# Four groups in seven-product form per pass of the two FFN output projections, instead of three

## The chip, the cores and the metric

The kernel runs on one core of a Trainium2 chip. The metric is the device time of one execution in microseconds; lower is better. The engines are TensorE (PE; its weight loads are listed as PEld), VectorE (DVE), ScalarE (ACT), GpSimd (POOL) and SyncE (SP, which here issues the weight DMAs).

## The reference

One decoder layer on 256 tokens of width 2048, in float32:

```
x = x + 0.5 * swiglu_ffn(rmsnorm(x), ffn1_w_in, ffn1_w_out)
h = rmsnorm(x); proj = h @ w_in        # two groups of 8 heads: q, k, v, and a forget gate
x = x + concat(dilated_attention(...), forgetting_attention(...)) @ w_out
x = x + 0.5 * swiglu_ffn(rmsnorm(x), ffn2_w_in, ffn2_w_out)

def swiglu_ffn(x, w_in, w_out):
    gate, up = jnp.split(x @ w_in, 2, axis=-1)
    return (jax.nn.silu(gate) * up) @ w_out
```

The hidden width of an FFN is 5504, which is 43 tiles of 128. The change touches only the product with `w_out`, 256 x 5504 by 5504 x 2048, in both FFNs.

## The kernel before

**Arithmetic.** Each float32 operand is split into a rounded part (hi, made by ScalarE's copy to fp32r) and the rest (lo, made by VectorE's subtraction), and every product is three matmuls: hi*hi, hi*lo, lo*hi. Weights come from HBM by DMA into `raw` slots of 8 KB per partition. ScalarE copies a half piece (128 x 1024) to `whi`, VectorE subtracts to get `wlo`, and TensorE uses both. There are four such slots; the unit of this chain is called a half here, and halves are numbered h. ScalarE may split half h only when TensorE has finished half h - 4 (`act_e.wait_ge(weights_used, h - SLOTS + 1)`).

**Output projection (`ffn_out` on each engine).** It runs in two passes of 1024 output columns. A pass is a list of items (`out_items`), one half each, in the same order on all engines. A `plain` item is one of the 43 activation tiles against its two 512 columns for both token blocks: 12 matmuls. A group takes four activation tiles as a 2 x 2 block matrix and computes its products in seven-product (Strassen-Winograd) form, one `form` item of 6 matmuls for each of T1, B11, T3, T2, B21, B22, T4. Four plain tiles cost 48 matmuls, one group 42. Before, each pass has 3 groups and 31 plain tiles. Within a group a plain item stands after B11, after T2 and after B22; `LEADS` says how many plain items stand ahead of each group: (8, 5, 5) in the first pass, (6, 5, 5) in the second.

**Additional work of a group.** VectorE makes four sums of weights in or from the group's two raw pieces (`out_sum`, 128 x 1024 each: T1's after the item two ahead of T1, T3's after T1, T2's after the item behind B11, T4's after the item behind T2). VectorE makes four sums of activations (`group_form_sums`, 128 x 256 each, after the item four ahead of T1), ScalarE rounds them (`group_form_hi`, 128 x 1024, ahead of the split three ahead of T1) and VectorE subtracts (`group_form_lo`). The group's own four activation tiles are split by `group_act_hi` (two ScalarE operations ahead of the split of the item before T1; waits until TensorE has used the previous group's T4) and `group_act_lo`. Each plain tile's activation is split by `act_hi` and `act_lo`, 128 x 256 each, into one of four tile places. At the end of a pass `join` adds the four separate product banks onto x, in steps 0 to 5, one after each item.

**Order.** All of it is written out by hand as program order per engine with semaphores. SyncE issues the loads in the order of `out_loads`; a raw slot is loaded again when `free(n)` says that its last reader is done. The group pieces use raw slots 3 and 4, the plain pieces 0 to 2, and slot 5 holds `sfo`, the split sums of the current group. The sums and their splits are made anew in the second pass. Between the FFNs the token mixer starts with `x_turn` (transposes of x) issued inside the last items of the second pass.

Of the kernel before, what the change touches and what calls it, by code (L numbers as in the profile page):

```python
# [7 lines left out]
P = 128  # L8
# [3 lines left out]
FT = D_FF // P  # L12
# [19 lines left out]
W = 512  # L32
UNITS = -(-D_FF // W)
# [39 lines left out]
PLAIN_TILES = FT - OUT_PLAIN  # L73

# [78 lines left out]
def layer(nc, io, out):  # L153
# [3 lines left out]
    with ctx:  # L157
# [9 lines left out]
        x = sb("x", [P, TB, D_MODEL])  # L167
        xs = sb("xs", [P, KT, 2, SEQ], f32r)
# [49 lines left out]
        place[0] = raw_at + 5 * 4 * W * 4  # L218
        sfo = sb("sfo", [P, 4, 2, 2, P], f32r)
        assert place[0] <= tsum_at  # L220
# [55 lines left out]
        def act_slot(c, k):  # L276
            return divmod((c * PLAIN_TILES + k) % 4, 2)

        def act_count(u, c, k):
            return PLAIN_TILES * (PASSES * u + c) + k - OUT_PLAIN + 1  # L280

# [10 lines left out]
        gs = [gset[:, 1 - c].rearrange("p b (f k t) -> p (b f) k t", f=2, k=2) for c in range(PASSES)]  # L292
# [35 lines left out]
        def _(sp):  # L328
            def free(n):
                for u in range(2):  # L330
# [138 lines left out]
        def _(pe):  # L469
# [112 lines left out]
            def ffn_out(u):  # L582
                for c in range(PASSES):
# [7 lines left out]
                    for i, item in enumerate(OUT_ITEMS[c][:ends]):  # L591
# [16 lines left out]
                        else:  # L608
                            g, f = item[1], item[2]
                            if f == "T1":  # L610
                                pe.wait_ge(gs_ready, group(u, c, g) + 1)
# [9 lines left out]
                            for k in range(2):  # L621
# [3 lines left out]
                                else:  # L625
                                    form_s = ("T1", "T2", "T3", "B22").index(f)
                                    st_hi, st_lo = sfo[:, form_s, k, 0, :], sfo[:, form_s, k, 1, :]
# [154 lines left out]
        def _(act_e):  # L782
# [57 lines left out]
            def act_hi(u, c, k):  # L840
                a, a_in = act_slot(c, k)
                act_e.wait_ge(act_copied, ACT_PAIRS * u + k // 2 + 1)
# [116 lines left out]
            def ffn_out(u):  # L959
                for c in range(PASSES):  # L960
                    for i, item in enumerate(OUT_ITEMS[c]):
# [4 lines left out]
                        if len(ahead) > 3 and ahead[3][0] == "form" and ahead[3][2] == "T1":  # L966
                            group_form_hi(u, c if i + 3 < OUT_LEN else c + 1, ahead[3][1])
# [147 lines left out]
        def _(dve):  # L1115
# [67 lines left out]
            def act_lo(u, c, k):  # L1183
                a, a_in = act_slot(c, k)
                dve.wait_ge(aw_hi_ready, act_count(u, c, k))
                V.tensor_tensor(aw_lo[:, a, a_in, :], act[:, k, :], aw_hi[:, a, a_in, :].bitcast(f32), ALU.subtract).then_inc(aw_ready, 1)
# [7 lines left out]
            def group_form_sums(u, c, g):  # L1194
                G, t, S = group(u, c, g), 4 * g, gs[c]
                A11, A21, A12, A22 = act[:, t:t + 2, 0:P], act[:, t:t + 2, P:2 * P], act[:, t + 2:t + 4, 0:P], act[:, t + 2:t + 4, P:2 * P]
                dve.wait_ge(act_copied, ACT_PAIRS * u + 2 * g + 2)
                dve.wait_ge(act_psum, UNITS * (u + 1) - 1 + c)
# [11 lines left out]
            def group_form_lo(u, c, g):  # L1210
                dve.wait_ge(gs_hi, group(u, c, g) + 1)
                V.tensor_tensor(sfo[:, :, :, 1, :], gs[c], sfo[:, :, :, 0, :].bitcast(f32), ALU.subtract).then_inc(gs_ready, 1)
# [19 lines left out]
            def join(u, c, step):  # L1232
# [10 lines left out]
                if step == 0:  # L1243
                    dve.wait_ge(p1_copied, PASSES * u + c + 1)
                    dve.wait_ge(gs_ready, group(u, c, OUT_GROUPS - 1) + 1)
# [127 lines left out]
            def ffn_out(u):  # L1373
                for c in range(PASSES):
                    t4 = OUT_ITEMS[c].index(("form", OUT_GROUPS - 1, "T4"))
                    for i, item in enumerate(OUT_ITEMS[c]):
# [5 lines left out]
                        if item[0] == "plain":  # L1382
                            k = item[1]
                            act_lo(u, c, k)
# [231 lines left out]
```

## Time and profile before

| | |
|---|---|
| time, median of 3 runs | 1767.82 us (1767.69 to 1769.09) |
| the profiled execution | 1767.65 us, span 1765.8 us |
| PE busy | 1759.1 us, 8062 matmuls |
| DVE busy | 1470.7 us (83%) |
| ACT busy | 1068.2 us (60%) |
| DMA | 350.84 MB, mean 199 GB/s |
| granted TensorE clock | 1.000 |

The span is the time from the first to the last instruction of the profile; the execution's own time is 1.85 us longer. A duration in a timeline is the time from issue to completion of one instruction, and neighbours on an engine overlap: the distance between starts is what an instruction costs a full engine.

### The profile page before, as it was taken

What the parts mean: (1) busy time and instruction counts of PE and PEld (TensorE: products, weight loads), DVE (VectorE), ACT (ScalarE), POOL (GpSimd) and SP (SyncE); (2) the same over time, 40 slices, a digit from 0 to 9 for tenths busy, and PEclk for the clock granted to TensorE, in tenths of its full rate; (3) what the DMA queues carried; (4) which work ended last, traced back from release to release, by engine and by line L of the source; (5) the groups of instructions that cost most, each with busy time, mean ns of one, the idle gap of its engine ahead of it and who ended that gap; (6) DMA issues with size and microseconds to landing.
All of it is one profiled execution on the core that took longest, in us unless ns stands there. A gap on an engine that the chain in (4) does not pass through costs nothing.

```text
span 1765.8 us, 20899 instructions
## 1 busy us (share of the span) xinstructions
PE 1759.1 (100%) x8062; PEld 1468.7 (83%) x8062; DVE 1470.7 (83%) x1624; ACT 1068.2 (60%) x1356; POOL 28.1 (2%) x34
## 2 busy tenths in 40 slices
PE   9999999999999999999999999999999999999999
PEld 7888888888988888888888888888888888988887
DVE  7999999998899998575655655999999999899988
ACT  7666666666666666454545554666666666666564
POOL 0000000000000001100000000000000000000000
PEclk9999999999999999999999999999999999999999
DMA  9655555554645546555455457355555555554662
GB/s 378 227 213 213 199 190 191 191 191 156 249 169 216 223 169 230 184 185 183 155 187 167 167 169 261 125 208 192 211 214 213 214 213 187 198 193 157 238 220 102
DMA packets 156179, 350.84 MB, mean 199 GB/s; under 512 B 5960, under 2 KB 16224, under 8 KB 155952
## 3 DMA queue, kind: packets, MB, share of 16 engines
q1 hardware_dynamic: 153280, 341.36, 54.8%
q0 software_dynamic: 1424, 5.53, 1.0%
q10 hardware_dynamic: 1376, 2.62, 0.4%
q8 instruction: 64, 1.05, 0.2%
q14 instruction: 35, 0.29, 0.0%
HBM read 347.37 MB, written 3.69 MB: 199 GB/s over the span
## 4 chain that ended last, share of the span: by engine, by line
PE 99%; DMA 0%; DVE 0%; ACT 0%; issue 0%; SPq 0%; ACTq 0%; DVEq 0%
PE bank L534 10%; PE bank L536 10%; PE bank L535 10%; PE bank L522 7%; PE bank L524 7%; PE bank L523 7%; PE bank L479 7%; PE bank L481 7%; PE bank L480 7%; PE bank L606 6%; PE bank L605 6%; PE bank L604 6%; PE bank L632 2%; PE bank L631 2%; PE bank L630 2%; PE bank L507 1%
## 5 line engine op out<-in xcount | busy, mean ns | idle before, releaser
L1120 DVE TENSOR_TENSOR wlo<-raw,whi 128x1024 fp32r<-128x1024 f32 (+1 forms) x644 | 764.9, 1206 | 190.3 <-ACT whi L791 185.8
L791 ACT ACTIVATE whi<-raw 128x1024 fp32r<-128x1024 f32 (+1 forms) x644 | 669.7, 1046 | 409.5 <-PE bank L481 191.6
L534 PE MATMUL bank<-whi,xs 128*128 128x512 f32 (+1 forms) x768 | 297.4, 387 | 1.5 <-DVE wlo L1120 1.5
L536 PE MATMUL bank<-whi,xs 128*128 128x512 f32 (+1 forms) x768 | 295.5, 385 | 0.0
L535 PE MATMUL bank<-wlo,xs 128*128 128x512 f32 (+1 forms) x768 | 295.3, 385 | 0.0
L604 PE MATMUL bank<-whi,aw_hi 128*128 128x512 f32 x484 | 188.7, 390 | 0.0
L606 PE MATMUL bank<-whi,aw_lo 128*128 128x512 f32 x484 | 188.4, 389 | 0.0
L605 PE MATMUL bank<-wlo,aw_hi 128*128 128x512 f32 x484 | 188.3, 389 | 0.0
L534 PEld LDWEIGHTS bank<-whi,xs 128*128 128x128 f32 x768 | 144.2, 188 | 29.1 <-issue 2.4
L536 PEld LDWEIGHTS bank<-whi,xs 128*128 128x128 f32 x768 | 144.1, 188 | 27.7
L535 PEld LDWEIGHTS bank<-wlo,xs 128*128 128x128 f32 x768 | 144.2, 188 | 26.8
L479 PE MATMUL bank<-whi,xs 128*128 128x512 f32 x384 | 155.8, 406 | 0.0
L481 PE MATMUL bank<-whi,xs 128*128 128x512 f32 x384 | 150.2, 391 | 0.0
L480 PE MATMUL bank<-wlo,xs 128*128 128x512 f32 x384 | 149.6, 390 | 0.0
L791 ACT ACTIVATE whi<-tsum 128x1024 fp32r<-128x1024 f32 (+1 forms) x80 | 83.0, 1040 | 96.5 <-PE bank L536 64.2
L524 PE MATMUL bank<-whi,sf 128*128 128x512 f32 (+1 forms) x320 | 122.7, 384 | 0.0
L522 PE MATMUL bank<-whi,sf 128*128 128x512 f32 (+1 forms) x320 | 122.7, 384 | 0.0
L523 PE MATMUL bank<-wlo,sf 128*128 128x512 f32 (+1 forms) x320 | 122.7, 384 | 0.0
L1120 DVE TENSOR_TENSOR wlo<-tsum,whi 128x1024 fp32r<-128x1024 f32 (+1 forms) x80 | 94.0, 1195 | 25.7 <-ACT whi L791 25.7
L606 PEld LDWEIGHTS bank<-whi,aw_lo 128*128 128x128 f32 x484 | 90.8, 188 | 18.8
L605 PEld LDWEIGHTS bank<-wlo,aw_hi 128*128 128x128 f32 x484 | 90.9, 188 | 18.8
L604 PEld LDWEIGHTS bank<-whi,aw_hi 128*128 128x128 f32 x484 | 90.8, 188 | 18.7
(195 smaller groups left out, 2579.7 us busy)
## 6 DMA issues: line engine op xcount, KB each, us to landing
raw<-ffn_w_in SPq DMA_DIRECT2D x158, 1024.0 KB, 7.1
raw<-ffn_w_out SPq DMA_DIRECT2D x84, 1024.0 KB, 6.7
raw<-w_in SPq DMA_DIRECT2D x48, 1024.0 KB, 5.0
raw<-w_out SPq DMA_DIRECT2D x16, 1024.0 KB, 5.0
raw<-ffn_w_in SPq DMA_DIRECT2D x16, 768.0 KB, 5.0
x<-x SPq DMA_DIRECT2D x4, 512.0 KB, 11.4
raw<-ffn_w_out SPq DMA_DIRECT2D x4, 512.0 KB, 4.2
xt<-x_turned SPq DMA_DIRECT2D x3, 512.0 KB, 8.6
```

The source lines that it names most:

```text
L479: mm(banks[b][:, 0:w], stationary[:, k, 0, tok], hi, start=k == 0, stop=False, skip_group_check=True)
L480: mm(banks[b][:, 0:w], stationary[:, k, 0, tok], lo, start=False, stop=False, skip_group_check=True)
L481: last = mm(banks[b][:, 0:w], stationary[:, k, 1, tok], hi, start=False, stop=k == k_total - 1, skip_group_check=True)
L522: mm(bank_out[:, 0:w], st_hi, hi, start=start and i == 0 and k == 0, stop=False, skip_group_check=True)
L534: mm(banks[b][:, 0:w], xs[:, k + i, 0, tok], hi, start=starts[b] and k + i == 0, stop=False, skip_group_check=True)
L535: mm(banks[b][:, 0:w], xs[:, k + i, 0, tok], lo, start=False, stop=False, skip_group_check=True)
L536: last = mm(banks[b][:, 0:w], xs[:, k + i, 1, tok], hi, start=False, stop=k + i == last_k, skip_group_check=True)
L604: mm(bank_out[:], st_hi, hi, start=i == 0, stop=False, skip_group_check=True)
L605: mm(bank_out[:], st_hi, lo, start=False, stop=False, skip_group_check=True)
L606: last = mm(bank_out[:], st_lo, hi, start=False, stop=k == FT - 1, skip_group_check=True)
L791: A(whi[:, h % SLOTS, 0:n_el], src, ACT.Copy).then_inc(weights_hi, 1)
L1120: V.tensor_tensor(wlo[:, h % SLOTS, 0:n_el], src, whi[:, h % SLOTS, 0:n_el].bitcast(f32), ALU.subtract).then_inc(weights_lo, 1)
```

## The change

Each pass has four groups and 27 plain tiles. The plain runs ahead of the groups become (4, 3, 2, 2) and (5, 2, 2, 2). The group pieces rotate over raw slots 3, 4 and 5, and a group's first piece is freed by the T4 sum, its second by the split of B22. `sfo` holds the split sums of all four groups and lies in the place of `xs`, which is idle in this stage; sums and splits are made in the first pass only, and the second reads them. `group_form_hi` therefore waits until TensorE has finished the last half of the input product (`weights_used` at OUT[u]). Plain activations are split two tiles at a time (128 x 512) into two places of two tiles, so `act_hi` waits for the tile three before; at the start of the second pass it waits for the last tile of the first. Two `join` steps of the second pass come behind its last item, and the two transposes of x stand behind the last two items.

```diff
-OUT_GROUPS = 3
+OUT_GROUPS = 4
-LEADS = ((8, 5, 5), (6, 5, 5))
+LEADS = ((4, 3, 2, 2), (5, 2, 2, 2))
+PLAIN_PAIRS = -(-PLAIN_TILES // 2)
@@ raw_slot
-            return 3 + q % 2 if q < 0 else (c * ACT_PLAIN + q) % 3
+            return 3 + (c * 2 * OUT_GROUPS + OUT_LOADS[c][i]) % 3 if q < 0 else (c * ACT_PLAIN + q) % 3
@@ layer
-        place[0] = raw_at + 5 * 4 * W * 4
-        sfo = sb("sfo", [P, 4, 2, 2, P], f32r)
+        place[0] = xs_at
+        sfo = sb("sfo", [P, OUT_GROUPS * 4, 2, 2, P], f32r)
@@
-            return divmod((c * PLAIN_TILES + k) % 4, 2)
+            return divmod((c * 2 * PLAIN_PAIRS + k - OUT_PLAIN) % 4, 2)
@@ sync: free(n)
-                        item = ("form", q // 2, "T4") if q < 2 * OUT_GROUPS else ("plain", min(2 * q + 1, FT - 1))
+                        if q < 2 * OUT_GROUPS and q % 2 == 0:
+                            return out_sums, 4 * group(u, c, q // 2) + 4
+                        item = ("form", q // 2, "B22") if q < 2 * OUT_GROUPS else ("plain", min(2 * q + 1, FT - 1))
@@ tensor: ffn_out
-                        if c and u == 0 and i in (OUT_LEN - 4, OUT_LEN - 2):
+                        if c and u == 0 and i >= OUT_LEN - 2:
                             pe.wait_ge(p_joined, 8 + 4)
-                            x_turn(1, (i - OUT_LEN + 4) // 2)
+                            x_turn(1, i - OUT_LEN + 2)
@@ scalar: act_hi(u, c, k)
+                n = min(2, FT - k)
                 if k >= OUT_PLAIN + 4:
-                    act_e.wait_ge(weights_used, out_half(u, c, ("plain", k - 4)) + 1)
+                    act_e.wait_ge(weights_used, out_half(u, c, ("plain", k - 3)) + 1)
                 elif c:
-                    act_e.wait_ge(weights_used, out_half(u, c - 1, ("plain", k - 4 + PLAIN_TILES)) + 1)
+                    act_e.wait_ge(weights_used, out_half(u, c - 1, ("plain", FT - 1)) + 1)
                 else:
                     act_e.wait_ge(weights_used, unit_half(u, UNITS - 1) + B22 + 2)
-                A(aw_hi[:, a, a_in, :], act[:, k, :], ACT.Copy).then_inc(aw_hi_ready, 1)
+                A(aw_hi[:, a, 0:n, :], act[:, k:k + n, :], ACT.Copy).then_inc(aw_hi_ready, 1)
@@ scalar: group_form_hi
-            def group_form_hi(u, c, g):
-                G = group(u, c, g)
-                if g or c:
-                    c0, g0 = (c, g - 1) if g else (c - 1, OUT_GROUPS - 1)
-                    act_e.wait_ge(weights_used, out_half(u, c0, ("form", g0, "B22")) + 1)
-                else:
-                    act_e.wait_ge(weights_lo, OUT[u])
-                act_e.wait_ge(gs_summed, 4 * G + 4)
-                A(sfo[:, :, :, 0, :], gs[c], ACT.Copy).then_inc(gs_hi, 1)
+            def group_form_hi(u, g):
+                act_e.wait_ge(weights_used, OUT[u])
+                act_e.wait_ge(gs_summed, 4 * (OUT_GROUPS * u + g + 1))
+                A(split_sums(g)[:, :, :, 0, :], gs, ACT.Copy).then_inc(gs_hi, 1)
@@ scalar: ffn_out
-                            act_hi(u, c, k)
+                            if (k - OUT_PLAIN) % 2 == 0:
+                                act_hi(u, c, k)
@@ vector: ffn_out
-                                if d == 3:
-                                    group_form_sums(u, c1, g1)
-                                if d == 2:
-                                    group_form_lo(u, c1, g1)
+                                if d == 3 and c1 == 0:
+                                    group_form_sums(u, g1)
+                                if d == 2 and c1 == 0:
+                                    group_form_lo(u, g1)
@@
+                for step in range(OUT_LEN - 1 - T4_ENDS[1], 6):
+                    join(u, 1, step)
```

## Rows read from the trace of the kernel before

**Rows 1.** The page, parts 1 and 2: the engines, and VectorE's share in 40 slices.

```profile
PE 1759.1 (100%) x8062; PEld 1468.7 (83%) x8062; DVE 1470.7 (83%) x1624; ACT 1068.2 (60%) x1356; POOL 28.1 (2%) x34
...
DVE  7999999998899998575655655999999999899988
```

**Rows 2.** The page, part 4: the chain that ended last.

```profile
PE 99%; DMA 0%; DVE 0%; ACT 0%; issue 0%; SPq 0%; ACTq 0%; DVEq 0%
```

**Rows 3.** Windows: stretch, length; PE, PEld, DVE, ACT, POOL, clock, DMA, GB/s; first pass.

```profile
461.30:574.70 113.40, 113.40 (x505) 93.91 (x504) 102.15 (x128) 70.32 (x94) 0.00 (x0) 1.00 0.55 204
```

**Rows 4.** Timeline of TensorE: start us, us, line, operation, tiles.

```profile
461.27 0.39 PE L604 MATMUL bank<-whi,aw_hi 128*128 128x512 f32 x1
...
483.76 0.39 PE L630 MATMUL bank<-whi,sfo 128*128 128x512 f32 x1
...
485.12 0.39 PE L630 MATMUL bank<-whi,aw_hi 128*128 128x512 f32 x1
...
574.20 0.39 PE L604 MATMUL bank<-whi,aw_hi 128*128 128x512 f32 x1
...
574.88 0.39 PE L604 MATMUL bank<-whi,aw_hi 128*128 128x512 f32 x1
```

**Rows 5.** Timeline of ScalarE, first FFN's output; [idle before <-releaser].

```profile
461.53 1.06 ACT L791 ACTIVATE whi<-raw 128x1024 fp32r<-128x1024 f32 x1 [0.71 <-PE bank L536]
...
467.03 1.06 ACT L791 ACTIVATE whi<-raw 128x1024 fp32r<-128x1024 f32 x1 [2.32 <-DMA raw<-ffn_w_out]
...
475.12 1.15 ACT L860 ACTIVATE aw_hi<-act 128x512 fp32r<-128x512 f32 x2
476.16 0.41 ACT L849 ACTIVATE aw_hi<-act 128x256 fp32r<-128x256 f32 x1
...
501.72 1.06 ACT L870 ACTIVATE sfo<-gset 128x1024 fp32r<-128x1024 f32 x1 [3.04 <-DVE gset L1208]
502.68 0.40 ACT L849 ACTIVATE aw_hi<-act 128x256 fp32r<-128x256 f32 x1
502.99 1.04 ACT L791 ACTIVATE whi<-raw 128x1024 fp32r<-128x1024 f32 x1
```

**Rows 6.** Timeline of VectorE, the same stretch.

```profile
461.69 0.61 DVE L1174 SCALAR_TENSOR_TENSOR gset<-bank,rstd,gset 128x384 f32<-128x384 f32 x1
...
463.33 0.42 DVE L1186 TENSOR_TENSOR aw_lo<-act,aw_hi 128x256 fp32r<-128x256 f32 x1
...
475.87 1.22 DVE L1120 TENSOR_TENSOR wlo<-raw,whi 128x1024 fp32r<-128x1024 f32 x1
477.01 1.22 DVE L1220 TENSOR_TENSOR tsum<-raw 128x1024 f32<-128x1024 f32 x1
...
479.62 1.28 DVE L1191 TENSOR_TENSOR aw_lo<-act,aw_hi 128x512 fp32r<-128x512 f32 x2
480.82 1.22 DVE L1393 TENSOR_TENSOR wlo<-tsum,whi 128x1024 fp32r<-128x1024 f32 x1
...
500.08 0.42 DVE L1203 TENSOR_TENSOR gset<-act 128x256 f32<-128x256 f32 x1
...
504.07 1.23 DVE L1120 TENSOR_TENSOR wlo<-raw,whi 128x1024 fp32r<-128x1024 f32 x1 [0.52 <-ACT whi L791]
```

**Rows 7.** Timeline of all engines at the start: TensorE's one wait for VectorE.

```profile
7.61 1.23 DVE L1120 TENSOR_TENSOR wlo<-raw,whi 128x1024 fp32r<-128x1024 f32 x1
...
8.98 0.47 PE L534 MATMUL bank<-whi,xs 128*128 128x512 f32 x1 [1.53 <-DVE wlo L1120]
...
9.28 0.39 PE L535 MATMUL bank<-wlo,xs 128*128 128x512 f32 x1
```

**Rows 8.** Timeline of ScalarE: the squares of x in the second pass.

```profile
592.42 0.62 ACT L816 ACTIVATE gset<-x 128x512 f32<-128x512 f32 x1
...
593.84 1.07 ACT L985 ACTIVATE whi<-raw 128x1024 fp32r<-128x1024 f32 x1
```

**Rows 9.** Timeline of SyncE: three loads issued at the start of the stage.

```profile
455.79 1.39 SPq L353 DMA_DIRECT2D raw<-ffn_w_out  x3
```

More of the change, by code:

```diff
@@ L167, in layer @@
         x = sb("x", [P, TB, D_MODEL])
+        xs_at = place[0]
         xs = sb("xs", [P, KT, 2, SEQ], f32r)
@@ L217, in layer @@
         assert place[0] <= tsum_at
-        place[0] = raw_at + 5 * 4 * W * 4
-        sfo = sb("sfo", [P, 4, 2, 2, P], f32r)
-        assert place[0] <= tsum_at
+        place[0] = xs_at
+        sfo = sb("sfo", [P, OUT_GROUPS * 4, 2, 2, P], f32r)
+        assert place[0] <= forms_at
         place[0] = tsum_at
@@ L276, in act_slot @@
         def act_slot(c, k):
-            return divmod((c * PLAIN_TILES + k) % 4, 2)
+            return divmod((c * 2 * PLAIN_PAIRS + k - OUT_PLAIN) % 4, 2)
         def act_count(u, c, k):
-            return PLAIN_TILES * (PASSES * u + c) + k - OUT_PLAIN + 1
+            return PLAIN_PAIRS * (PASSES * u + c) + (k - OUT_PLAIN) // 2 + 1
         def group(u, c, g):
@@ L290, in pair, with split_sums @@
             return tile.rearrange("p (k f) -> p k f", k=2)
-        gs = [gset[:, 1 - c].rearrange("p b (f k t) -> p (b f) k t", f=2, k=2) for c in range(PASSES)]
+        gs = gset[:, 1].rearrange("p b (f k t) -> p (b f) k t", f=2, k=2)
+        def split_sums(g):
+            return sfo[:, 4 * g:4 * g + 4]
         p_banks = [bank[0:4], bank[4:8]]
@@ L610, in ffn_out @@
                             if f == "T1":
-                                pe.wait_ge(gs_ready, group(u, c, g) + 1)
+                                pe.wait_ge(gs_ready, OUT_GROUPS * u + g + 1)
                                 if g == 0 and c == 0:
@@ L626, in ffn_out @@
                                     form_s = ("T1", "T2", "T3", "B22").index(f)
-                                    st_hi, st_lo = sfo[:, form_s, k, 0, :], sfo[:, form_s, k, 1, :]
+                                    st_hi, st_lo = split_sums(g)[:, form_s, k, 0, :], split_sums(g)[:, form_s, k, 1, :]
                                 hi, lo = whi[:, slot, k * W:(k + 1) * W], wlo[:, slot, k * W:(k + 1) * W]
@@ L840, in act_hi @@
             def act_hi(u, c, k):
+                n = min(2, FT - k)
                 a, a_in = act_slot(c, k)
[L842 removed]
+                act_e.wait_ge(act_copied, ACT_PAIRS * u + (k + n - 1) // 2 + 1)
                 if k >= OUT_PLAIN + 4:
[L844 removed]
+                    act_e.wait_ge(weights_used, out_half(u, c, ("plain", k - 3)) + 1)
                 elif c:
[L846 removed]
+                    act_e.wait_ge(weights_used, out_half(u, c - 1, ("plain", FT - 1)) + 1)
                 else:
                     act_e.wait_ge(weights_used, unit_half(u, UNITS - 1) + B22 + 2)
[L849 removed]
+                A(aw_hi[:, a, 0:n, :], act[:, k:k + n, :], ACT.Copy).then_inc(aw_hi_ready, 1)
             def group_act_hi(u, c, g):
@@ L965, in ffn_out @@
                             act_copy(u, UNITS - 1)
-                        if len(ahead) > 3 and ahead[3][0] == "form" and ahead[3][2] == "T1":
-                            group_form_hi(u, c if i + 3 < OUT_LEN else c + 1, ahead[3][1])
+                        if c == 0 and i + 3 < OUT_LEN and ahead[3][0] == "form" and ahead[3][2] == "T1":
+                            group_form_hi(u, ahead[3][1])
                         if len(ahead) > 1 and ahead[1][0] == "form" and ahead[1][2] == "T1":
@@ L1183, in act_lo @@
             def act_lo(u, c, k):
+                n = min(2, FT - k)
                 a, a_in = act_slot(c, k)
                 dve.wait_ge(aw_hi_ready, act_count(u, c, k))
-                V.tensor_tensor(aw_lo[:, a, a_in, :], act[:, k, :], aw_hi[:, a, a_in, :].bitcast(f32), ALU.subtract).then_inc(aw_ready, 1)
+                V.tensor_tensor(aw_lo[:, a, 0:n, :], act[:, k:k + n, :], aw_hi[:, a, 0:n, :].bitcast(f32), ALU.subtract).then_inc(aw_ready, 1)
             def group_act_lo(u, c, g):
@@ L1192, in group_act_lo, with group_form_sums @@
                                     ALU.subtract).then_inc(ga_ready, 1)
-            def group_form_sums(u, c, g):
-                G, t, S = group(u, c, g), 4 * g, gs[c]
+            def group_form_sums(u, g):
+                G, t, S = OUT_GROUPS * u + g, 4 * g, gs
                 A11, A21, A12, A22 = act[:, t:t + 2, 0:P], act[:, t:t + 2, P:2 * P], act[:, t + 2:t + 4, 0:P], act[:, t + 2:t + 4, P:2 * P]
                 dve.wait_ge(act_copied, ACT_PAIRS * u + 2 * g + 2)
-                dve.wait_ge(act_psum, UNITS * (u + 1) - 1 + c)
+                dve.wait_ge(act_psum, UNITS * (u + 1) - 1)
                 if G:
@@ L1208, in group_form_sums, with group_form_lo @@
                 V.tensor_tensor(S[:, 3], A12, S[:, 1], ALU.subtract).then_inc(gs_summed, 1)
-            def group_form_lo(u, c, g):
-                dve.wait_ge(gs_hi, group(u, c, g) + 1)
-                V.tensor_tensor(sfo[:, :, :, 1, :], gs[c], sfo[:, :, :, 0, :].bitcast(f32), ALU.subtract).then_inc(gs_ready, 1)
+            def group_form_lo(u, g):
+                dve.wait_ge(gs_hi, OUT_GROUPS * u + g + 1)
+                V.tensor_tensor(split_sums(g)[:, :, :, 1, :], gs, split_sums(g)[:, :, :, 0, :].bitcast(f32), ALU.subtract).then_inc(gs_ready, 1)
             def out_sum(u, c, g, f):
@@ L1244, in join @@
                     dve.wait_ge(p1_copied, PASSES * u + c + 1)
-                    dve.wait_ge(gs_ready, group(u, c, OUT_GROUPS - 1) + 1)
+                    dve.wait_ge(gs_ready, OUT_GROUPS * (u + 1))
                     V.tensor_tensor(u2, P6[:], p1s[:], ALU.add).then_inc(p_joined, 1)
@@ L1383, in ffn_out @@
                             k = item[1]
-                            act_lo(u, c, k)
+                            if (k - OUT_PLAIN) % 2 == 0:
+                                act_lo(u, c, k)
                             n = out_piece(u, c, k // 2)
```

## The prediction

> **What bounds the kernel now.** I read the engines' shares first: TensorE is busy for 1759.1 of 1765.8 us, VectorE for 83% over all, but 90% or more in most slices of the FFNs' stages [rows 1]. The chain that ended last is 99% TensorE [rows 2], so a matmul taken out is worth its whole distance to the next, as long as weights arrive in time. Next I took the stage that changes, by its first pass: 113.40 us in which TensorE never rests while VectorE is busy for 102.15 [rows 3]. So VectorE has 10% to spare here, no more. Last come the timelines of the engines, for distances between starts. TensorE: a form item of 6 matmuls takes 485.12 - 483.76 = 1.36 us, three matmuls 0.68, so a plain item of 12 takes 2.72 and a matmul 0.227 [rows 4]. (31 plain and 21 form items make 112.9; the pass has 0.5 more, its six transposes [rows 3].) VectorE: 1.14 for a 1024-wide operation, 0.60 for a 512-wide one [rows 6]. ScalarE: 0.96 and 0.52 [rows 5].
>
> Four latencies decide the rest. TensorE's next item starts at 461.27 and ScalarE, released by the last one, at 461.53: 0.26 [rows 4, 5]. From the start of ScalarE's split to that of VectorE's: 504.07 - 502.99 = 1.08 [rows 5, 6]. From the start of VectorE's split to the first matmul that waited for it: 8.98 - 7.61 = 1.37 [rows 7]. And the round trip of the activation sums: VectorE starts them at 500.08, ScalarE rounds at 501.72 (1.64), its next operation starts 0.96 later, VectorE's next split 1.08 after that: 3.68 in which VectorE does 1.5 us of work [rows 5, 6].
>
> **The saving.** Four passes have each one group more: 6 matmuls less in each, 24 x 0.227 = 5.4 us. ScalarE and VectorE also lose the second pass's activation sums and their splits; neither engine bounds that pass, so this is worth nothing by itself.
>
> **First pass: VectorE becomes the bound.** Between two T1's that are one lead of 2 apart VectorE has 12 splits, 4 weight sums and the split of the activation sums (17 x 1.14 = 19.4), 2.5 pairs of plain activations (1.5), the group's own (1.2) and the round trip (3.7): 25.8 us. TensorE needs 7 x 1.36 + 5 x 2.72 = 23.1. With a lead of 5 it was 20 such operations, eight single tiles of activation (about 0.34 each), 1.2 and 3.7: 30.4 against 31.3, and it just fitted. A lead of 2 does not fit, and four halves of buffer can't carry it, the less as the stage now begins late: ScalarE must wait for the last matmul of the input product before it rounds the first sums, ahead of item 1. The split of item 1 so starts on VectorE 0.26 + 0.96 + 1.08 = 2.3 after the stage begins. From there VectorE has work without a gap. Up to the split of P36 (item 43, the plain tile behind B11 of the last group; behind it come no more sums of activations, and VectorE gets ahead) these are 42 splits, 4 splits of sums, 14 weight sums (60 x 1.14 = 68.4), 10 pairs (6.0), 4 group activations (4.8), 3 round trips (11.0), the SwiGLU of the last unit (1.6 [rows 6]) and 0.6 where it waits for ScalarE: 92.4. TensorE can start P36 at 2.3 + 92.4 + 1.4 = 96.1. Unhindered it would be there after 20 plain and 23 form items and the transposes: 86.2. So 9.9 us are lost per first pass, 19.8 in all. If VectorE did not bind, only waits that begin at TensorE would be left in this pass: 1.0 at item 1 (2.3 + 1.4 - 2.7) and some 2 at each of two groups, 5.0; that is the lower bound. I take 9.9, since every term is a row of this stage.
>
> **Start of the second pass.** The first pair of activations now waits for P42, the item just ahead. ScalarE sees its end after 0.26, rounds the pair (0.52), splits the weights (1.08 to VectorE), and VectorE's split takes 1.37 to the first matmul: 3.2 us of idle TensorE where there was none, as the old wait was for the tile four before. Twice 6.5. Queued behind that wait on ScalarE are the splits of the next items; they are made during the first item's 2.72 and are not late. No buffer needs this wait (P42's tile lies in the other place), but the program has it.
>
> **Lead of 2 in the second pass.** `group_act_hi` waits for the previous T4, and only one plain item runs behind that T4 before the item whose weights are queued behind it on ScalarE. From T4's end: 0.26 + 1.04 (two operations [rows 5]) + 1.08 + 1.37 = 3.75 against 2.72: 1.0 lost. Where this item also starts a pair (second of the three such groups) 0.52 more. Then VectorE, held up, is late again: B11's split starts 4.6 after the late one (split, group activations, T1, T3's sum), B11 is ready at 6.0, TensorE there at 5.45: 0.5; and where the next plain item has a pair, 0.4 more. 1.95 + 2.1 + 1.95 = 6.0 per second pass, 12.0 for both. The lower bound is 0, if TensorE already runs late there for another reason; I take 12, as VectorE needs only 20.9 us per 23.1 in that pass.
>
> **Small ones.** x's squares in the second pass (1.4 on ScalarE [rows 8]) now stand behind T2, ahead of the split of P22: 0.8, first FFN only. The transposes of x come one item later, so that the mixer's first weights, queued on ScalarE behind the rounding of x, are some 0.4 late. At the very end the single tile P42 may be rounded only when P39 is used: 0.26 + 0.40 + 0.42 and latencies, 1.2, then 0.4 for its weights. The two late `join` steps fit into the last 9 matmuls: nothing. After a wait the second matmul comes at 9.28 - 8.98 = 0.30 instead of 0.227 [rows 7]; over some 14 waits that VectorE's pace does not swallow, 1.0. Together 3.8; bounds 0 and 8.
>
> **DMA.** Three loads issued together at 455.79 let the third be used at 467.03, 11.2 us later [rows 5, 9]. At a lead of 2 the two pieces of a group and a plain piece start in the same way after P27's split, and T1's sum comes 12.2 us after (8 x 1.14 + 0.6 + 3.7 less the split itself). Covered by 1.0. For the first group the old order already has the pieces there by then. I count nothing.
>
> **The sum.** 19.8 + 6.5 + 12.0 + 3.8 = 42.1 lost, 5.4 saved: +36.7. On the profiled execution's 1767.65 (0.2 below the median of the runs) this is 1804.3; I say 1804.
>
> **Rivals.** (1) VectorE does not bind: its order overlaps better than my walk has it. For it speaks that the old pass had no wait; against it the 25.8 to 23.1. Then 9.8 less: 1794. Chance 0.13. (2) Supply holds everywhere but for the start of the second pass, which is a wait on the item just ahead and can't be hidden: -5.4 + 6.5, 1769. Chance 0.05. (3) The other side: weights and activations come in time in spite of all this and the saving stands, 1762. It would need VectorE 11% faster in the first pass and the boundary's wait be met before TensorE runs dry; it decides only if a 1.14 us operation is in truth shorter when the engine is full, and the rows are from a full engine. Chance 0.06. (4) The clock. Rows show 1.00 granted throughout this pass [rows 3] and no gap of TensorE there; the longest gap is the 1.53 at the start [rows 7]. The two gaps of 3.2 are new. If the clock falls to 1.2 GHz behind each, then one or two items at twice the distance add 2.7 to 5.4 us each time: 1809 to 1815. Chance 0.06. The Trainium skill (TensorE: Matmul & The Clock Gate, "HAM oscillation") holds that long enough idle gaps throttle TensorE again; it is this rival's rule, and no row of this trace has a gap like that. (5) The three loads take 3 us longer than the row, so that T1's sum waits 2 us at four of the eight groups or more: +8, 1812. Chance 0.04. The forecast itself has 0.66.
>
> Under 0.2% (3.5 us) a measurement of this kernel can't be told from no change. Faster 0.06 (rival 3), same 0.06 (rival 2 and a little of the forecast's tail), slower 0.88. The forecast's own range is 1796 to 1812; with rivals 1, 4 and 5 and the bounds 1787 to 1814.
>
> **What would show it.** In the profile after: 24 matmuls fewer, TensorE idle for about 42 us, mostly put down to VectorE's `wlo`; VectorE busy without a gap from item 1 to the last group of each first pass except for the round trips; a first pass of about 113.4 - 1.4 + 9.9 = 121.9; a gap of 3.2 us at the start of each second pass; gaps of 1.0, 1.5, 1.0 two items behind T4 in it. Wrong if TensorE has no idle time in the first pass, if the boundary shows none, or if the granted clock falls.

## The result

The changed kernel takes 1810.57 us (median of 5 runs, 1807.17 to 1811.15) against 1767.71 us (5 runs) for the kernel before: ratio 1.0235, 95% interval 1.0224 to 1.0246, slower. The forecast was 1804, with a range of 1787 to 1814: +36.7 us forecast on the profiled execution, +43.0 measured (1810.65, span 1808.9). The matmuls are 24 fewer (8038), as the change says. All times here are medians; one execution of the first experiment below, 2204.88 us in the chip's slow state, is left out.

The page of the kernel after, parts 1, 2 and 4 (beside [rows 1] and [rows 2]):

```profile
PE 1772.9 (98%) x8038; PEld 1463.7 (81%) x8038; DVE 1489.3 (82%) x1572; ACT 1066.1 (59%) x1304; POOL 28.1 (2%) x34
...
DVE  6999999998897889575655555999999998889787
...
PE 89%; DVE 7%; ACT 2%; DMA 1%; issue 1%; ACTq 0%; SPq 0%; DVEq 0%
```

TensorE now rests for 36.0 us of the span (1808.9 - 1772.9), where it rested for 6.7 (1765.8 - 1759.1); its busy time is 13.8 us longer although there are 24 matmuls fewer, because a slow matmul and a short wait count as busy there. The chain holds VectorE for 7% where it held none. The waits (engine, line waited for, by whom released: us in total, times, longest):

```profile
PE bank L612 <- DVE wlo L1125: 20.6, 20, 3.1
PE bank L638 <- DVE wlo L1400: 4.6, 14, 0.6
...
ACT aw_hi L858 <- PE bank L614: 35.7, 8, 6.8
ACT aw_hi L869 <- PE bank L640: 32.7, 10, 4.3
ACT sfo L874 <- PE bank L544: 10.2, 2, 5.1
...
DVE tsum L1226 <- DMA raw<-ffn_w_out: 7.9, 3, 4.6
```

TensorE waits for `wlo`; behind it ScalarE waits for TensorE, 35.7 us for places of plain tiles, 32.7 for the previous T4, 10.2 for the last matmul of the input product. Windows of the first FFN (stretch, length; PE, PEld, DVE, ACT, POOL, clock, DMA share, GB/s), in order the first pass, the gap behind it, what follows the gap, and as the last row what follows the same gap in the second FFN:

```profile
462.90:585.00 122.10, 116.31 (x499) 91.51 (x497) 107.24 (x116) 70.50 (x82) 0.00 (x0) 1.00 0.51 191
585.00:588.20 3.20, 0.13 (x1) 0.02 (x1) 2.06 (x3) 2.97 (x5) 0.00 (x0) 1.00 0.66 270
588.20:592.60 4.40, 4.39 (x12) 3.48 (x13) 4.40 (x6) 3.00 (x5) 0.00 (x0) 0.61 0.32 115
...
1682.20:1688.00 5.80, 5.80 (x14) 4.54 (x15) 5.80 (x8) 2.98 (x5) 0.00 (x0) 0.50 0.54 167
```

The first pass, 113.4 us in [rows 3], takes 122.1 with VectorE at 107.24 of it. Behind it TensorE stands still for 3.2 us, and then the granted clock is 0.61 and 0.50 where [rows 3] had 1.00. The gaps by themselves, from TensorE's timeline:

```profile
466.46 0.47 PE L612 MATMUL bank<-whi,aw_hi 128*128 128x512 f32 x1 [0.69 <-DVE wlo L1125]
...
521.43 0.50 PE L638 MATMUL bank<-whi,aw_hi 128*128 128x512 f32 x1 [0.62 <-DVE wlo L1400]
...
523.80 0.47 PE L612 MATMUL bank<-whi,aw_hi 128*128 128x512 f32 x1 [0.69 <-DVE wlo L1125]
...
550.39 0.47 PE L612 MATMUL bank<-whi,aw_hi 128*128 128x512 f32 x1 [1.31 <-DVE wlo L1125]
...
559.00 0.47 PE L612 MATMUL bank<-whi,aw_hi 128*128 128x512 f32 x1
...
588.21 0.47 PE L612 MATMUL bank<-whi,aw_hi 128*128 128x512 f32 x1 [3.08 <-DVE wlo L1125]
...
589.35 0.63 PE L613 MATMUL bank<-wlo,aw_hi 128*128 128x512 f32 x1
589.77 0.63 PE L614 MATMUL bank<-whi,aw_lo 128*128 128x512 f32 x1
...
625.07 0.47 PE L612 MATMUL bank<-whi,aw_hi 128*128 128x512 f32 x1 [0.83 <-DVE wlo L1125]
629.68 0.47 PE L638 MATMUL bank<-whi,aw_hi 128*128 128x512 f32 x1 [0.27 <-DVE wlo L1400]
...
650.70 0.47 PE L612 MATMUL bank<-whi,aw_hi 128*128 128x512 f32 x1 [1.35 <-DVE wlo L1125]
...
675.44 0.47 PE L612 MATMUL bank<-whi,aw_hi 128*128 128x512 f32 x1 [0.83 <-DVE wlo L1125]
...
1746.35 0.47 PE L612 MATMUL bank<-whi,aw_hi 128*128 128x512 f32 x1 [1.99 <-DVE wlo L1125]
...
1796.41 0.50 PE L660 MATMUL bank<-whi,aw_hi 128*128 128x512 f32 x1 [1.03 <-DVE aw_lo L1192]
```

466.46 is item 1, late behind ScalarE's wait for the input product. 521.43 to 550.39 are waits by VectorE's pace; 559.00 is P36. 588.21 is the start of the second pass: 588.21 less 584.74, the start of the last matmul before, less 0.227 is 3.24 us. The next matmuls stand 0.42 apart (589.35 to 589.77), not 0.23 as in [rows 4]. 625.07, 650.70 and 675.44 are the three leads of 2 in the second pass, 629.68 the B11 behind the first of them; 1746.35 is the middle one in the second FFN, 1796.41 the last tiles of all. (Where a row gives less idle time than the distance of starts does, the previous matmul's end is counted in; below I use distances of starts less 0.227.)

VectorE in the first pass, the three longest pauses behind the split of item 1:

```profile
494.06 1.23 DVE L1125 TENSOR_TENSOR wlo<-raw,whi 128x1024 fp32r<-128x1024 f32 x1 [2.14 <-ACT whi L799]
...
520.15 1.23 DVE L1400 TENSOR_TENSOR wlo<-tsum,whi 128x1024 fp32r<-128x1024 f32 x1 [2.13 <-ACT whi L990]
...
546.14 1.23 DVE L1400 TENSOR_TENSOR wlo<-tsum,whi 128x1024 fp32r<-128x1024 f32 x1 [2.14 <-ACT whi L990]
```

These are the round trips of the activation sums of the second, third and fourth group.

The chain at the second pass's start, ScalarE and VectorE:

```profile
585.23 0.63 ACT L858 ACTIVATE aw_hi<-act 128x512 fp32r<-128x512 f32 x1 [6.79 <-PE bank L614]
585.76 1.99 ACT L799 ACTIVATE whi<-raw 128x1024 fp32r<-128x1024 f32 x2
...
586.83 1.23 DVE L1125 TENSOR_TENSOR wlo<-raw,whi 128x1024 fp32r<-128x1024 f32 x1 [0.25 <-ACT whi L799]
```

ScalarE has waited 6.79 us for TensorE's last tile, rounds the pair, splits at 585.76; VectorE follows 1.07 later, TensorE 1.38 after that.

### The profile page after: what moved, and what is told of

It reads as the page before. It is cut to its first block, busy times and chain, and to the rows that moved or that the text cites. A ratio compares the mean times of both kernels' runs of the same rounds, so it can differ in the third digit from the quotient of the medians.

```text
span 1808.9 us, 20673 instructions
## 1 busy us (share of the span) xinstructions
PE 1772.9 (98%) x8038; PEld 1463.7 (81%) x8038; DVE 1489.3 (82%) x1572; ACT 1066.1 (59%) x1304; POOL 28.1 (2%) x34
## 4 chain that ended last, share of the span: by engine, by line
PE 89%; DVE 7%; ACT 2%; DMA 1%; issue 1%; ACTq 0%; SPq 0%; DVEq 0%
PE bank L542 10%; PE bank L544 9%; PE bank L543 9%; PE bank L530 7%; PE bank L532 7%; PE bank L531 7%; PE bank L487 6%; PE bank L489 6%; PE bank L488 6%; PE bank L612 4%; PE bank L613 3%; PE bank L614 3%; PE bank L638 2%; DVE wlo L1400 2%; DVE wlo L1125 2%; PE bank L640 2%
## 5 line engine op out<-in xcount | busy, mean ns | idle before, releaser
L1125 DVE TENSOR_TENSOR wlo<-raw,whi 128x1024 fp32r<-128x1024 f32 (+1 forms) x628 | 745.2, 1206 | 204.8 <-ACT whi L799 199.6
L799 ACT ACTIVATE whi<-raw 128x1024 fp32r<-128x1024 f32 (+1 forms) x628 | 651.5, 1045 | 389.4 <-PE bank L489 188.4
L612 PE MATMUL bank<-whi,aw_hi 128*128 128x512 f32 x420 | 168.5, 401 | 21.8 <-DVE wlo L1125 20.6
L613 PE MATMUL bank<-wlo,aw_hi 128*128 128x512 f32 x420 | 165.5, 394 | 0.0
L614 PE MATMUL bank<-whi,aw_lo 128*128 128x512 f32 x420 | 165.4, 394 | 0.0
L990 ACT ACTIVATE whi<-raw 128x1024 fp32r<-128x1024 f32 x80 | 84.6, 1059 | 70.3 <-DVE raw L1233 41.6
L612 PEld LDWEIGHTS bank<-whi,aw_hi 128*128 128x128 f32 x420 | 79.8, 190 | 50.4 <-issue 34.7
L1400 DVE TENSOR_TENSOR wlo<-raw,whi 128x1024 fp32r<-128x1024 f32 x80 | 96.1, 1219 | 0.0
## 6 DMA issues: line engine op xcount, KB each, us to landing
x<-x SPq DMA_DIRECT2D x4, 512.0 KB, 12.2
```

The costliest lines, as they stand in the source:

```text
L612: mm(bank_out[:], st_hi, hi, start=i == 0, stop=False, skip_group_check=True)
L799: A(whi[:, h % SLOTS, 0:n_el], src, ACT.Copy).then_inc(weights_hi, 1)
L1125: V.tensor_tensor(wlo[:, h % SLOTS, 0:n_el], src, whi[:, h % SLOTS, 0:n_el].bitcast(f32), ALU.subtract).then_inc(weights_lo, 1)
```

## The experiments

Each was timed beside the kernel before on the same chip; its medians lie between 1767.5 and 1769.0, so each time is also given as a ratio with its interval. Where a pass is measured, it is the distance from its first matmul to its last one's end: 122.1 us in the changed kernel's first passes, and 112.2 (113.6 before, less 1.4) if nothing holds TensorE up.

**The wait at the second pass's start.**

```diff
-                    act_e.wait_ge(weights_used, out_half(u, c - 1, ("plain", FT - 1)) + 1)
+                    act_e.wait_ge(weights_used, out_half(u, c - 1, ("plain", FT - 2 if k == OUT_PLAIN else FT - 1)) + 1)
```

> The first activation pair of the second pass waits for the tile that last used its place (P41), no longer for P42; all else as in the changed kernel. My theory: the idle time of TensorE at the start of each second pass is this wait, and the matmuls at half clock behind it are its consequence. Then the gap falls from 3.25 us to 3.23 - 2.72 = 0.5 us, no matmul behind it is at the lower clock, and the time falls by 2 x 2.7 + some 4 us to about 1801. Rival (VectorE or the loads are late there by themselves): the gap stays near 3 us, time 1809 to 1811.

1800.49 us, ratio 1.0187 (1.0170 to 1.0204), 10.1 less than the changed kernel. The gap, and one that is new:

```profile
585.47 0.47 PE L612 MATMUL bank<-whi,aw_hi 128*128 128x512 f32 x1 [0.37 <-DVE wlo L1125]
...
607.88 0.47 PE L612 MATMUL bank<-whi,aw_hi 128*128 128x512 f32 x1 [0.24 <-DVE wlo L1125]
```

The gap is 0.53 us by distance of starts and the matmuls behind it stand 0.23 apart. So the wait on the tile just ahead makes the gap, and without the long gap the clock didn't fall here. The new gap, 0.40 us, stands ahead of P22, where the squares of x are: they cost nothing only as long as TensorE is late anyway. The reverse, the same wait put into the kernel before:

```diff
-                    act_e.wait_ge(weights_used, out_half(u, c - 1, ("plain", k - 4 + PLAIN_TILES)) + 1)
+                    act_e.wait_ge(weights_used, out_half(u, c - 1, ("plain", FT - 1 if k == OUT_PLAIN else k - 4 + PLAIN_TILES)) + 1)
```

> The kernel before with one word changed: the first activation of the second pass waits for the last tile of the first pass instead of the tile four before. My theory: this alone costs its chain, twice 0.26 + about 0.35 + 1.08 + 1.37 = 3.1, and the lower clock behind it, 1.6 to 2.9 each: +9 to +12, 1777 to 1779. Rival (the gap needs the late VectorE of the changed kernel): below 1770.

1780.87 us, ratio 1.0068 (1.0054 to 1.0081):

```profile
577.84 0.77 PE L604 MATMUL bank<-whi,aw_hi 128*128 128x512 f32 x1 [2.86 <-DVE wlo L1120]
...
577.80:584.00 6.20, 6.16 (x15) 4.87 (x16) 6.17 (x12) 1.74 (x3) 0.00 (x0) 0.51 0.48 166
```

One wait, with VectorE in time everywhere, costs a gap of 3.02 us in each FFN, and the second pass behind it is longer by 2.95 us in the first FFN (15 matmuls in 6.1 us in place of 3.4) and by 2.85 in the second (8 matmuls at half rate, 1.6, and two gaps of 0.4 that follow). That is the 11.8 us by which the profiled execution is longer, within the expected 9 to 12. The median is 12.8 above the kernel before in its round (1768.03); what the other executions lost beyond the profiled one isn't shown.

**Three groups, all else as changed.**

```diff
-OUT_GROUPS = 4
+OUT_GROUPS = 3
-LEADS = ((4, 3, 2, 2), (5, 2, 2, 2))
+LEADS = ((8, 5, 5), (6, 5, 5))
```

> Three groups per pass with the old leads (8, 5, 5) and (6, 5, 5), but with all else of the change: kept split sums in the place of xs, pairs of activations, rotating pieces, later transposes. My theory: what the first pass and the lead of 2 lose comes from the dense groups, not from the new storage; only the second pass's start (3.2 us each and the clock behind it, some 11 us) and the tail (1.6) remain: about 1780, no idle TensorE in the first pass. Rival (the new storage, the shared splits or the pairs cost by themselves): first pass with idle TensorE, 1795 or more.

1780.76 us, ratio 1.0077 (1.0060 to 1.0094). In the first passes TensorE has no gap at all; each FFN has one at its boundary (the last row is the window behind the second):

```profile
578.14 0.47 PE L612 MATMUL bank<-whi,aw_hi 128*128 128x512 f32 x1 [3.08 <-DVE wlo L1125]
...
1658.51 0.47 PE L612 MATMUL bank<-whi,aw_hi 128*128 128x512 f32 x1 [3.08 <-DVE wlo L1125]
...
1658.50:1664.50 6.00, 5.99 (x26) 4.97 (x27) 6.00 (x8) 2.16 (x4) 0.00 (x0) 1.00 0.53 176
```

Behind the second of them the clock stayed at 1.00, though the gap is as long as the first; the lower clock is likely behind such a gap, not certain. Kept sums, pairs and rotating slots cost nothing in the passes: what is left is the boundary (6.5, and 1.7 for the clock), the tail (1.5) and the mixer's late start (1.1), 10.8 of the profiled execution's 11.2. The other 30 us of the change are the fourth group and the short leads.

**The round trip.** ScalarE rounds and VectorE subtracts the activation sums one item later:

```diff
-                        if c == 0 and i + 3 < OUT_LEN and ahead[3][0] == "form" and ahead[3][2] == "T1":
-                            group_form_hi(u, ahead[3][1])
+                        if c == 0 and i + 2 < OUT_LEN and ahead[2][0] == "form" and ahead[2][2] == "T1":
+                            group_form_hi(u, ahead[2][1])
...
-                                if d == 2 and c1 == 0:
+                                if d == 1 and c1 == 0:
                                     group_form_lo(u, g1)
```

> The changed kernel with ScalarE's rounding of the activation sums and VectorE's subtraction one item later, so that VectorE splits one more item while the sums are rounded. My theory: VectorE's pace bounds the first pass and 2.2 us of each group is its wait in the round trip; without it TensorE's idle time in a first pass falls from 8.6 us to about 4 (the waits that begin at TensorE), and the late item 1 goes: 9 us less in all, about 1802. Rival (VectorE's pace is not the bound, the waits on the previous T4 are): 2 us less at most, 1809.

1801.11 us, ratio 1.0193 (1.0178 to 1.0208), 9.5 less than the changed kernel. The first passes last 118.0 and 118.1 us in place of 122.1, 8.1 less for both; 1.7 more is the start of the kernel, which was not at the lower clock in this execution as it was in the changed kernel's (see below). Two of the gaps left begin at the previous T4, with the sizes that the second pass has. The third row and the window behind it are from the second FFN's second pass:

```profile
522.05 0.47 PE L612 MATMUL bank<-whi,aw_hi 128*128 128x512 f32 x1 [1.35 <-DVE wlo L1125]
...
546.77 0.47 PE L612 MATMUL bank<-whi,aw_hi 128*128 128x512 f32 x1 [0.80 <-DVE wlo L1125]
...
1735.46 0.47 PE L612 MATMUL bank<-whi,aw_hi 128*128 128x512 f32 x1 [2.17 <-DVE wlo L1125]
...
1737.20:1740.20 3.00, 3.00 (x8) 2.35 (x8) 3.00 (x4) 0.38 (x1) 0.00 (x0) 0.50 0.00 0
```

In the changed kernel the first two were hidden behind VectorE's pace. (The third is the middle lead of 2 with its late load; here the lower clock followed a gap of 2.3 us.)

**VectorE's load taken away instead**, weight sums in the first pass an eighth as wide:

```diff
+                narrow = 64 if c == 0 else W
-                B11, B12, B21, B22 = quarter(n0, 0), quarter(n0, 1), quarter(n1, 0), quarter(n1, 1)
+                B11, B12, B21, B22 = (q[:, :, 0:narrow] for q in (quarter(n0, 0), quarter(n0, 1), quarter(n1, 0), quarter(n1, 1)))
```

> The changed kernel with the four weight sums of each group 64 columns wide per tile instead of 512 in the first pass (work left out: the other columns are not summed), so VectorE has some 0.9 us less per sum and 14 us less per first pass, its waits and order unchanged. My theory: the first pass is bound by VectorE's pace, so of its 8.6 us of idle TensorE only what begins at TensorE stays, the late item 1 (1.3 with its sequel) and the waits on T4 (some 4): 5 to 6, time 1804 to 1806. Rival (fixed latencies, not VectorE's load): idle time unchanged at 8 to 9, time 1810.

1797.86 us, ratio 1.0169 (1.0155 to 1.0183), 12.7 less than the changed kernel where 4.6 to 6.6 were expected. The first passes last 117.1 us each in place of 122.1: 10.0 less for both, with 4.8 each still lost, close to the prediction's lower bound of 5.0. In the profiled execution 1.6 us more come again from the start of the kernel, and 1.2 from the clock behind the second boundary. Both ways to give VectorE time back, less work and a shorter round trip, shorten the first pass: its load and its round trip together are the bound.

**The wait on the previous T4.**

```diff
+            def group_act_hi(u, c, g, part):
-                    act_e.wait_ge(weights_used, out_half(u, c0, ("form", g0, "T4")) + 1)
+                    act_e.wait_ge(weights_used, out_half(u, c0, ("form", g0, ("B11", "T4")[part])) + 1)
...
+                        if item[0] == "form" and item[2] == "T3":
+                            group_act_hi(u, c, item[1], 1)
```

> The changed kernel with the group's own activation split in two parts: the first half, which only B11 reads, waits for the previous B11; the second, read from B21 on, is made behind B11 and waits for the previous T4. My theory: the wait for T4 two items ahead costs 5.3 us of idle TensorE per second pass and some 1 to 2 in the first; all of it in the second pass goes: 11 to 14 us less, about 1798. Rival (these gaps are VectorE's pace): the gaps stay, 1808 or more.

1794.54 us, ratio 1.0153 (1.0138 to 1.0168), 16 less than the changed kernel where 11 to 14 were expected; 1.7 of it is again the start of the kernel. From the boundary's gap to the end of the second pass of the first FFN TensorE has no gap; in the second FFN one of 1.4 us stays, by a late load. The first passes still last 121.0 and 121.1 us, held up by VectorE:

```profile
519.63 0.50 PE L638 MATMUL bank<-whi,aw_hi 128*128 128x512 f32 x1 [1.07 <-DVE wlo L1402]
...
548.08 0.47 PE L612 MATMUL bank<-whi,aw_hi 128*128 128x512 f32 x1 [1.29 <-DVE wlo L1127]
```

**All mendings together**, with the weights split ahead of a late activation, each last tile waited for by itself and the transposes of x one item earlier:

```diff
+                            late = k == FT - 1 or (c and k == OUT_PLAIN)
+                            if (k - OUT_PLAIN) % 2 == 0 and not late:
+                                act_hi(u, c, k)
...
+                            if late:
+                                act_hi(u, c, k)
```

> The changed kernel with four mendings together: the place-true wait at the second pass's start with the weights split ahead of that activation, the round trip one item later, the group's activation in two parts, the last tile waited for by itself, and the transposes of x one item earlier. My theory: all waits that I name are gone and VectorE needs 23.5 us for 23.1 at a lead of 2 in the first pass, which the buffer carries, so the 5.4 us of matmuls show: 1763, at most 1 to 2 more: 1762 to 1766. Rival (late loads of the group pieces bind next, as T1's sum waited for them three times): up to 5 more, 1768.

1772.78 us, ratio 1.0026 (1.0016 to 1.0035): 7 us above the expected range. Two things were left. VectorE's sum for T1 waits for its pieces at a lead of 2, so that the plain item behind it on VectorE is late (times as in the waits above, then TensorE's gap in the second FFN's first pass), and VectorE's pace still lengthens the first passes, 116.1 and 117.2 us in place of 112.2:

```profile
DVE tsum L1230 <- DMA raw<-ffn_w_out: 6.1, 4, 3.6
...
1598.18 0.47 PE L612 MATMUL bank<-whi,aw_hi 128*128 128x512 f32 x1 [2.15 <-DVE wlo L1129]
```

**Loads in another order.** Each group's first piece two plain pieces earlier, its second ahead of the plain piece:

```diff
+            back = 0 if g == 0 and c == 0 else 1
+            first.setdefault(max(i - 2 * back, 0), []).append(2 * g)
+            second.setdefault(i - back, []).append(2 * g + 1)
...
-        for g in at.get(i, []):
-            loads += [2 * g, 2 * g + 1]
+        loads += first.get(i, []) + second.get(i, [])
```

> The mended kernel with each group's first piece loaded two plain pieces earlier and its second ahead of the plain piece it stood behind. My theory of the 8 us by which the mended kernel missed: VectorE's sum for T1 waits for the group's pieces (6.1 us in four waits), which puts 4.6 us of idle on TensorE, and the rest is VectorE's pace in the first pass. Then these four waits go and the time falls from 1772.8 to 1768 to 1769. Rival (the loads are late for want of bandwidth, not of order): the waits only move to plain pieces, 1772.

1769.87 us, ratio 1.0013 (1.0004 to 1.0022). No sum waits for a load any more; 2.9 us went, not the 4 to 5 expected, as the first of these gaps stays by VectorE's pace. The second passes now lose nothing; the first ones last 116.1 us each, 3.9 lost:

```profile
521.36 0.47 PE L617 MATMUL bank<-whi,aw_hi 128*128 128x512 f32 x1 [1.01 <-DVE wlo L1134]
```

**VectorE's sums on GpSimd**, on top of that (`group_form_sums` moved to GpSimd's program, same operations):

```diff
-                V.tensor_tensor(S[:, 0], A21, A22, ALU.add).then_inc(gs_summed, 1)
+                pool.tensor_tensor(S[:, 0], A21, A22, ALU.add).then_inc(gs_summed, 1)
```

> The same with the four activation sums of each group made by the idle GpSimd instead of VectorE, as early as their buffer is free. My theory: VectorE has 1.5 us less per group and no round trip, 22.0 us of work per 23.1 of TensorE at a lead of 2, so the first pass keeps some 0.5 us of idle TensorE: 1765 to 1766, below the kernel before. Rival (GpSimd's sums on the shared buffer are slow or hold up VectorE): sums later than ScalarE wants them, 1768 or more.

1773.92 us, ratio 1.0035 (1.0023 to 1.0048): slower, as the rival had it. The group of the third sum (busy us, mean ns of one); VectorE's splits beside the first four sums, the same splits in the run without the move, and the gap of TensorE that follows:

```profile
L461 POOL TENSOR_TENSOR gset<-gset,act 128x256 f32<-128x256 f32 x8 | 10.8, 1348 | 0.0
...
436.23 5.75 DVE L1154 TENSOR_TENSOR wlo<-raw,whi 128x768 fp32r<-128x768 f32 x4
...
434.51 3.84 DVE L1134 TENSOR_TENSOR wlo<-raw,whi 128x768 fp32r<-128x768 f32 x4
...
444.57 0.44 PE L555 MATMUL bank<-whi,xs 128*128 128x384 f32 x1 [1.22 <-DVE wlo L1154]
```

One such sum takes 1.35 us on GpSimd and 0.42 on VectorE; four in a row are 5.0 to 6.1 us. And VectorE is slower beside them: its 128x768 splits take 1.49 us each in place of 0.95, its 128x1024 splits 1.76 in place of 1.22. Ahead of each output stage this puts a gap of 1.3 us on TensorE (444.57, and 1521.28 in the second FFN) that the run without the move doesn't have. Inside a first pass ten operations of VectorE are 0.54 us longer, 5.4 in all, which is more than the three rounds of sums (3 x 1.5) taken from it: the pass lasts 115.8 us in place of 116.1. So this run doesn't test a lighter VectorE. The rest of the 4 us is the start of the kernel, which was at the lower clock in this profiled execution (1.7 us).

**Subtraction later**, on top of the loads (one item on, just ahead of `group_act_lo`), **and then another lead** on top of both.

```diff
-                                if d == 1 and c1 == 0:
-                                    group_form_lo(u, g1)
...
+                                    if c1 == 0:
+                                        group_form_lo(u, g1)
```

> e9_loads_earlier with VectorE's subtraction of the split activation sums moved behind the split of the item before T1. In e9_loads_earlier TensorE is idle for 2.9 us per first pass, 1.2 of it ahead of the plain item before the third group's T1, which stands on VectorE behind that subtraction and T1's weight sum, with no load late. My theory: VectorE's order and pace; this gap shrinks by its 1.1 to nearly nothing and half of it comes back ahead of T1: 1 to 2 us less in all, 1768 to 1769. Rival (VectorE's amount of work alone counts): the same 1769.9.

1770.04 us, ratio 1.0011 (1.0003 to 1.0020): the rival's, and the first passes last 116.1 us as before this edit. The gap went from the plain item (521.36) to B11 behind T1:

```profile
525.27 0.47 PE L643 MATMUL bank<-whi,aw_hi 128*128 128x512 f32 x1 [0.65 <-DVE wlo L1412]
```

```diff
-LEADS = ((4, 3, 2, 2), (5, 2, 2, 2))
+LEADS = ((4, 3, 3, 2), (5, 2, 2, 2))
```

> e11_form_lo_later with leads (4, 3, 3, 2) in the first pass, so that one more plain item stands ahead of the third group and three instead of four behind the last. My theory: the pace there becomes 24.9 us of VectorE against 25.8 of TensorE; only the start of the stage and the last lead of 2 keep idle time, about 1.5 per first pass, 3 in all against 5.4 saved: 1766, below the kernel before by 1 to 2 us. Rival (each group costs its own wait whatever its lead): 1769.

1768.37 us, ratio 1.0000 (0.9991 to 1.0009): no difference from the kernel before, and not the 1766 expected. The first passes last 114.9 us, 2.7 lost each where 1.5 were expected. The gap at the third group is gone, the one at the last lead of 2 stays:

```profile
551.37 0.47 PE L643 MATMUL bank<-whi,aw_hi 128*128 128x512 f32 x1 [0.64 <-DVE wlo L1412]
```

So four groups can be carried at the cost of three, and no version here beat the kernel before.

## Why the prediction was right

The direction, the engine and the places were those forecast; the size was 6 us short. By the two traces the 43.0 us are 1.6 ahead of the first output stage, 8.5 + 3.2 + 5.8 in its first pass, boundary and second pass, 2.2 between the stages, and 8.5 + 3.2 + 10.0 in the second stage. The page shows 29.3 us more of idle TensorE (36.0 less 6.7), not the 42 that I named as a sign; the rest lies inside its busy time. By its steps (measured: distances of starts, first FFN / second FFN):

- **The saving**, 5.4: 24 matmuls at 0.227. With the waits mended and the loads reordered, the second passes last 113.34 and 111.54 us against 114.70 and 112.88 before: 1.36 and 1.34 less, six matmuls each.
- **First pass**, 9.9 lost each: from the stage's first matmul (462.85) to the last one's end (584.97) are 122.1 us, against 113.6 (574.88 - 461.27 [rows 4]) - 1.4 unhindered: 9.9, and 9.8 in the second FFN. Item 1 came 0.85 late (0.95 forecast), VectorE paused three times for 2.1 us, each time in a round trip, and the last late item was P36, at 559.00, 96.15 after the stage's start (96.1 walked). The step that named VectorE's pace stands by two experiments (round trip, 4.1 less per pass; light sums, 5.0 less). Its lower bound, 5.0 lost with VectorE no bound, is near the 4.8 that light sums left.
- **Start of the second pass**, 3.2: 3.24 and 3.24.
- **Lead of 2 in the second pass**, 6.0: 1.7 + 1.9 + 1.7 = 5.3, and 5.9 in the second FFN, where the middle one was 0.6 longer by a late load of T1's pieces (VectorE waited 4.63 us for it). Splitting the wait took all of it away but for the late load.
- **Small ones.** The squares of x, 0.8 forecast, cost nothing here, since TensorE was already late at P22; where the boundary's wait was mended they cost 0.40. The mixer's first weights were 0.5 late (0.4), and a second gap of 0.7 stands at 716.28, ahead of the mixer's next transposes of x; I had it as nothing. The tail: 1.2 + 0.3 (1.6). The second matmul behind a wait, late by 0.06 to 0.12 each time: 1.6 in both second passes (1.0).
- **The clock**, nothing in the sum. This is the term that was off. Behind each of the two 3.2 us gaps the clock fell to its level of 1.2 GHz: 12 matmuls in 4.4 us instead of 2.8 the first time, 14 in 6.0 instead of 3.2 the second, together 4.4 us. The rival I gave 0.06 came true beside the forecast, not in place of it, as it should have been written: it depends on the gaps that the forecast makes. The forecast itself had named a falling clock as a sign of being wrong, and that sign came. Its price is from these rows. The Trainium skill (TensorE: Matmul & The Clock Gate, "HAM oscillation") holds that long enough idle gaps throttle TensorE again, and this trace agrees at both of its 3.2 us gaps.
- **The start of the kernel**, not in the sum either: in this execution the clock was already lower behind the first wait, 0.86 between 9 and 20 us, and the output stage began 1.6 us later than before for it. The change touches nothing there, and the runs that share this start had it in one profiled execution and not in the next (at the first output stage 462.86 in the boundary's run, 461.16 in the run with the wait on T4 split), so these 1.6 us are not the change's.

```profile
9.00:20.00 11.00, 10.93 (x42) 8.94 (x43) 10.04 (x16) 9.32 (x16) 0.00 (x0) 0.86 1.06 403
```

- **DMA**, nothing: right for TensorE at 15 of the 16 sums for T1. Three of VectorE's sums waited 7.9 us in all (645.90, 1714.84 and 1743.24), and the last of them reached TensorE. All three stand in second passes, and there the step was wrong: its 12.2 us contain the round trip of 3.7, which the second pass no longer has. Without it the sum stands 8.5 us behind the loads by VectorE's work alone, against the 11.2 that [rows 5] and [rows 9] give for three loads. Late loads became the next bound when the rest was mended.

36.7 + 4.4 (clock) + 1.6 (start of the kernel) + 0.8 (mixer: 1.2 for 0.4) + 0.6 (second matmuls) - 0.8 (squares) - 0.7 (leads of 2: 11.3 for 12.0, the late load included) - 0.1 (first passes) - 0.1 (tail) is 42.4 of the measured 43.0; the rest is in distances that are a few ns longer behind waits.

Of the rivals, that VectorE does not bind, that only the boundary costs, and that the saving stands are refuted by the first pass's gaps. Late loads alone are not it: one of 16 reached TensorE, for 0.6 us.

## What to carry to other kernels

A matmul saved on the engine that bounds is only worth something while the engines that feed it keep the new pace: divide their work between two marks by the matmul time between the same marks, the round trips included, and 25.8 to 23.1 says before any code is written that the pace can't be kept. When a buffer is regrouped, check each wait it changes for how many items ahead of its use it lies; a wait on the item just ahead exposes the whole chain, and in this kernel mostly also brought the lower clock. An idle gap of this length should be priced with the clock behind it, as one term and not as a rival. Work moved to an idle engine can slow the engine that it was to relieve: here GpSimd's sums took as much from VectorE as they gave.

## What the hardware showed beside that

- Inside the output stages there are twelve gaps of TensorE of 3.0 to 3.2 us (two each in the changed kernel, the kernel before with the wait, three groups, the round trip, light sums and the split wait on T4). Matmuls at half rate followed eleven of them, 6 to 14 each time, for 1.3 to 2.9 us; they did not follow the second one of the three-group run. Of five gaps of 2.1 to 2.3 us one was followed by them (1735.46 in the run of the round trip), and none of the shorter ones in these stages. So the length of the gap alone doesn't decide it.
- At the start of the kernel the first wait took 1.1 to 2.7 us in the thirteen profiled executions, and the clock fell behind it in three of them (behind 2.38, 2.08 and 2.06 us), not behind 2.72, 2.53 or 2.40. It cost 1.6 to 1.7 us. The kernel before's own executions lie near 1767.5 and near 1769.2 us, which would fit this, but none of the slower ones was profiled.
- A 128x256 float32 sum took 1.35 us on GpSimd and 0.42 on VectorE, and while GpSimd made such sums VectorE's splits of 128x1024 took 1.76 us in place of 1.22.
